# Order of the gates, the recurrence and the item table in a mixer and expert layer

## The reference

```
mod = silu(c) @ ada_w + ada_b                      # 1024 x 6144, six rows of 1024
z   = rmsnorm(x) * (1 + sc1) + sh1
xa, ya, u, v = split(z @ w_in, 4)                  # each 1024 x 512
xc  = causal_conv4(xa) + conv_b
r, i = sigmoid(xc @ wr + br), sigmoid(xc @ wi + bi)   # per head of 64 channels
a   = exp(-8 * r * softplus(-lambda))
h_t = a_t * h_(t-1) + sqrt(1 - a_t^2) * i * xc     # scan over the 1024 tokens
o_lru = h * gelu(ya)
o_sgu = gelu(u) * (W_causal @ layernorm(gelu(v)) + b)
h   = x + g1 * (concat(rmsnorm(o_lru), rmsnorm(o_sgu)) @ w_out)
z2  = rmsnorm(h) * (1 + sc2) + sh2
top4, gates = router(z2)
moe = sum over the four experts e of gate * (swiglu(z2 @ w_gu[e]) @ w_down[e])
out = rmsnorm(h + g2 * moe)
```

## Time and profile before

| what | us |
|---|---|
| median of 3 runs (lowest to highest) | 2106.76 (2106.14 to 2109.04) |
| the profiled run, whole | 2113.14 |
| its span, first to last instruction | 2111.4 |
| TensorE busy | 1947.7 (92%) |
| TensorE busy from 0 to 50 / 50 to 100 us | 14.92 / 46.92 |
| TensorE busy from 150 to 200 / 200 to 250 us | 42.42 / 43.13, granted clock 0.93 / 0.90 |
| TensorE busy from 450 to 500 / 500 to 550 us | 28.32 / 38.23, granted clock 0.79 / 0.86 |
| VectorE, ScalarE, GpSimd busy | 1007.5, 355.6, 536.5 |
| VectorE's first part of the table, end (`places_made`) | 479.4 |
| moved by DMA | 527.20 MB, mean 250 GB/s; from 0 to 54.68 us 329 GB/s |

### The profile page before, as it was taken

How to read it: one execution, slowest core, us unless ns; L and a number is a source line. 1 busy time by engine, 2 the same in 40 slices (tenths; PEclk the granted TensorE clock), 3 DMA queues, 4 the chain that set the end, 5 groups by cost and what they waited for, 6 DMA issues and landing times.

```text
span 2111.4 us, 53224 instructions
## 1 busy us (share of the span) xinstructions
PE 1947.7 (92%) x20253; PEld 805.0 (38%) x20254; DVE 1007.5 (48%) x2278; ACT 355.6 (17%) x729; POOL 536.5 (25%) x536
## 2 busy tenths in 40 slices
PE   3998999986889989999999999999999999999994
PEld 2443444441333424334343333343333333334332
DVE  6427756334534434544454544545444454454444
ACT  3024411221111111101010111111111111111012
POOL 2000022112232232322222323323333233322231
PEclk9998999997999999999999999999999999999997
DMA  9332135323492591959696969789898898999985
GB/s 327 137 119 80 40 120 172 153 92 130 131 362 83 185 358 25 347 201 337 208 332 214 376 252 389 274 329 359 283 392 287 305 354 285 389 397 356 332 297 180
DMA packets 128957, 527.20 MB, mean 250 GB/s; under 512 B 17184, under 2 KB 47920, under 8 KB 79760
## 3 DMA queue, kind: packets, MB, share of 16 engines
q1 hardware_dynamic: 95344, 470.39, 57.8%
q0 software_dynamic: 33568, 56.29, 11.5%
HBM read 494.22 MB, written 32.38 MB: 249 GB/s over the span
## 4 chain that ended last, share of the span: by engine, by line
PE 72%; DMA 15%; DVE 5%; SPq 4%; ACT 2%; issue 1%; POOL 1%; DVEq 0%; ACTq 0%; POOLq 0%
PE psum L1198 38%; PE psum L1218 20%; DMA big<-in_exp_w_gu_dram 10%; PE psum L1115 5%; PE psum L959 5%; DMA big<-in_exp_w_down_dram 2%; PE psum L1052 2%; SPq L487 1%; DMA big<-in_w_in_dram 1%; PE psum L999 1%; SPq L497 1%; DVE big L1409 1%; PE psum L1159 1%; SPq L468 0%; SPq L494 0%
## 5 line engine op out<-in xcount | busy, mean ns | idle before, releaser
L1198 PE MATMUL psum<-big,r 128*32 128x512 f32 x9152 | 1011.4, 599 | 39.1 <-DMA big<-in_exp_w_gu_dram 28.3
L1198 PEld LDWEIGHTS psum<-big,r 128*32 128x32 f32 x9152 | 291.4, 111 | 711.4 <-issue 649.9
L1218 PE MATMUL psum<-big,r 128*32 128x256 f32 x9152 | 511.1, 383 | 10.2 <-DVE r L1838 8.0
L689 POOL DMA_INDIRECT acc_rows<-r,scatter_idx x143 | 226.9, 1587 | 858.3 <-DVE r L1848 830.1
L1218 PEld LDWEIGHTS psum<-big,r 128*32 128x32 f32 x9152 | 293.9, 111 | 206.0 <-DVE r L1838 11.1
L870 ACT ACTIVATE r<-r,shift 128x128 f32<-128x128 f32 x376 | 154.2, 481 | 912.8 <-PE psum L1198 852.7
L678 POOL DMA_INDIRECT r<-hs_rows,gather_idx x192 | 223.7, 1165 | 87.7 <-issue 45.8
L1845 DVE TENSOR_TENSOR r<-psum,r 128x256 f32<-128x256 f32 x143 | 60.8, 425 | 288.0 <-PE psum L1218 287.0
L1823 DVE TENSOR_TENSOR r<-psum,r 128x256 f32<-128x256 f32 x143 | 60.4, 422 | 270.8 <-PE psum L1198 270.8
L959 PE MATMUL psum<-r,big 128*128 128x512 f32 x384 | 167.7, 597 | 3.1 <-DMA big<-in_w_in_dram 3.1
L1776 DVE STREAM_TRANSPOSE r<-r 128x1024 f32<-128x1024 f32 x47 | 97.6, 2076 | 107.8 <-issue 107.8
(11 more groups left out here) (286 smaller groups left out, 927.9 us busy)
## 6 DMA issues: line engine op xcount, KB each, us to landing
big<-in_exp_w_gu_dram SPq DMA_DIRECT2D x256, 1024.0 KB
big<-in_exp_w_down_dram SPq DMA_DIRECT2D x128, 1024.0 KB
big<-in_ada_w_dram SPq DMA_DIRECT2D x12, 2048.0 KB, 12.9
r<-in_x_dram SPq DMA_DIRECT2D x16, 512.0 KB, 12.7
big<-in_w_in_dram SPq DMA_DIRECT2D x4, 2048.0 KB, 20.2
r<-in_exp_b_gu_dram SPq DMA_DIRECT2D x128, 64.0 KB
big<-in_w_out_dram SPq DMA_DIRECT2D x2, 2048.0 KB, 13.4
hs_rows<-r POOLq DMA_DIRECT2D x8, 512.0 KB, 2.9
```

The source lines that it names most:

```text
L689: pool.indirect_dma_start(acc_quarters, bass.IndirectOffsetOnAxis(ap=scatter_idx[:, u:u + 1], axis=0), y_sb[:, u, :], None, bounds_check=4 ...
L1198: last = pe.matmul(psum[32 * j:32 * j + 32, u, :].rearrange("p (a n) -> p a n", a=2), izT[:, k, u * UNIT:(u + 1) * UNIT], rhs[:, :, 256 * ...
L1218: ins_ = pe.matmul(psum[32 * i:32 * i + 32, 4 + u % 2, 0:256], actT[:, u, f, :], down_slab(f)[:, 256 * i:256 * i + 256], start=(f == 0), s ...
```

## The change

Two stretches are written in another order, and the table chain gets shorter. No product of TensorE's main work is added or removed.

**Front.** The eleven small parameter loads go from SyncE's queue to ScalarE's. The gates' weights get a semaphore of their own (`gatew_in`) and, with all other mixer parameters of GpSimd's queue, are issued after `zT`, where before most of them were issued behind the third block of products. The two stores of zeros go behind the masking of `wmT`. `gates(0)` stands behind the second pair of `xa` projections, `gates(1)` behind the fourth, `gates(2)` behind the second pair of `ya`, `gates(3)` behind the fourth. The scan writes to `xaT` and no longer to `lru_t`, and the product with `ya` is a step of its own (`apply`), so that the recurrence doesn't need `ya`.

**Way in.** `make_places` comes ahead of the first unit's products. The second part of the table chain starts right after it, with the transpose of unit 0 behind its first four instructions; three sums at a time are taken with one instruction over a three-part tile, so that the chain has 33 instructions with the transpose among them, where it had 42 without it. `make_items` comes after the first unit's last pass. The table is copied out before the transposes of units 1 to 3. TensorE loads two of four registers later, waits for only one half of the modulated rows, and makes list 4 before `first_2b`. In the loop `make_onehot` comes right behind `block_rows`.

The diff, cut to its core:

```
@@ bank_jobs @@
+    for m in range(CT):
+        jobs += [("xa", (m, th), "dve") for th in range(2)]
+        if m % 2:
+            jobs += gates(m // 2)
...
     for ct in range(CT):
         jobs += [("ya", (ct, th), "act") for th in range(2)]
-        if ct >= 1:
-            jobs += gates(ct - 1)
+        if ct % 2:
+            jobs += gates(2 + ct // 2)
@@ SyncE: the loop over PARAM_ROWS goes away; ScalarE gets it as its first work @@
+            for name, rows in PARAM_ROWS:
...
+                act.dma_start(prow[ROW[name]:ROW[name] + rows, :], src.rearrange(pat, p=P)).then_inc(param_in, SEMW)
@@ GpSimd @@
-            pool.wait_ge(gemv_made, 3)
+            pool.wait_ge(filled, JOB[("zT", (KT - 1, 1))] + 1)
             for s in range(2):
                 for bd, w in ((wr_bd, "lru_wr"), (wi_bd, "lru_wi")):
...
-                                   ins[w][0].rearrange("(c s) i o -> s i c o", s=2)[s]).then_inc(mixpar_in, SEMW)
+                                   ins[w][0].rearrange("(c s) i o -> s i c o", s=2)[s]).then_inc(gatew_in, SEMW)
@@ TensorE @@
+            for m in range(CT):
+                for th in range(2):
+                    project("xa", ("win", 0), m, th)
+                if m == 1:
+                    pe.wait_ge(gatew_in, SEMW * 4)
+                if m % 2:
+                    gates(m // 2)
...
+            make_places()
             pe.wait_ge(first_made[0], 1)
-            gate_and_linear(0, 0, first=True, between=lambda k: make_places() if k == 0 else None)
+            gate_and_linear(0, 0, first=True)
             pe.wait_ge(first_made[1], 1)
-            gate_and_linear(0, 1, first=True, between=lambda k: make_items() if k == 2 else None)
+            gate_and_linear(0, 1, first=True, between=lambda k: make_items() if k == 3 else None)
             pe.wait_ge(items_ready, 1)
...
+            load_word(0, 1)
+            pe.reg_alu(units, loaded[1], 1, ALU.max)
+            pe.reg_mov(arrived, SEMW)
+            pe.wait_ge(z_made[0], 1)
...
             by_units(pe, units, 3, first_3b)
+            make_list(4, release=(freed[3],))
             by_units(pe, units, 2, first_2b)
-            make_list(4, release=(freed[3],))
+            repeat_rows(4)
             by_units(pe, units, 1, first_1b)
@@ VectorE, recurrence @@
-                link(dve.tensor_tensor_scan(lru_t[:, 0, :], lru_t[:, 3, :], lru_t[:, 2, :], 0.0, ALU.mult, ALU.add))
-                dve.tensor_tensor(yaT[:, ct, :], yaT[:, ct, :], lru_t[:, 0, :], ALU.mult).then_inc(lru_made, 1)
+                dve.tensor_tensor_scan(xaT[:, ct, :], lru_t[:, 3, :], lru_t[:, 2, :], 0.0, ALU.mult, ALU.add
+                                       ).then_inc(lru_made, 1)
...
+            copy_xa(0)
+            conv(0)
+            mod_products(4)
+            copy_xa(1)
+            mod_products(5)
+            recurrence(0)
+            conv(1)
+            copy_xa(2)
+            copy_xa(3)
...
+            recurrence(1)
+            conv(2)
+            mod_products(6)
+            apply(0)
+            apply(1)
+            recurrence(2)
+            conv(3)
+            apply(2)
+            mod_add(6)
+            mod_products(7)
+            recurrence(3)
+            apply(3)
@@ VectorE, table: one of the two sums over a three-part tile @@
+            link(dve.tensor_tensor(chosen, at_place, mask.unsqueeze(1).broadcast_to([P, 3, NE]), ALU.mult))
+            link(dve.tensor_reduce(sums_b, chosen, AX.X, ALU.add))
@@ VectorE, loop @@
                 block_rows(g + 1)
+                make_onehot(g + 3)
                 rows_here(g + 4, step)
                 make_idx(g + 2, step)
                 make_gates(g + 2, step)
-                make_onehot(g + 3)
```

More of the change, by code:

```diff
@@ L97, in bank_jobs @@
         if m == 0:
-            jobs += gates(CT - 1) + [("mod", 7, "dve")]
+            jobs += [("mod", 7, "dve")]
         if m == 2:
@@ L992, in _ @@
                 last.then_inc(filled, 1)
-            def gates(ct):
-                pe.wait_ge(conv_made, ct + 1)
-                for name, w in (("rec", wr_bd), ("inp", wi_bd)):
-                    for th in range(2):
-                        b = open_bank(name, (ct, th))
-                        pe.matmul(b, w[:, ct, :], lru_t[:, 0, th * 512:(th + 1) * 512], start=True, stop=True
-                                  ).then_inc(filled, 1)
             def sum_squares(grp, th):
```

157 lines of the change are left out of this document (72 added, 85 removed).

## The result

The changed kernel takes 2078.39 us, the median of four runs (2070.52 to 2079.87), beside 2106.45 (2105.9 to 2109.04) for the kernel before, four runs on the same chip. The ratio of the two is 0.985, 95% interval 0.983 to 0.987. Forecast were 2074.0 us, range 2067 to 2083. On two other chips the ratio came out at 0.985 and 0.985 again.

A forecast was written before the change was run, and what follows sets the result against it. TensorE, busy 92% of the span, was taken as the bound, so only its waits and starts pay. 22.2 + 2.5 + 3.4 + 4.7 = 32.8 us off the median 2106.8 gave 2074.0 us, range 2067 to 2083.

The forecast's parts named there:

- Front: Projections to the end of u: gates stop waiting, 14.5 us of waits and 7.7 of slowed passes go, 22.2 us gained.
- slow passes: In the front, gate passes and the last pair of u run slower after waits; 7.7 us expected to go with the waits.
- Opening: Start to first projection: w_in leaves the path, VectorE's chain starts sooner; gain 2.5 us, between a loss of 1.1 and 3.8.
- rule of turns between rings: Parameter loads at the start: DMA engines alternate between rings packet by packet, so landing is small and the sum 1.3 us better.
- Way in to unit 1: From the first unit to unit 1's first pass: no wait in `make_items`, four modulations awaited instead of eight; 3.4 us gained.
- rule of the exclusive lock: Table chain beside GpSimd's gates: shared SBUF ports held for a whole instruction; by it alone the 3.4 us gain could be 0.
- First down product: Behind unit 1's start: earlier list 4 and one-hot matrix, register loads overlapped; 4.7 us gained, 2.7 if loads don't overlap.
- Loop: Items of the loop: earlier one-hot matrix counts 0, since TensorE then waits for the next expert's weights; at best 4 us.
- rival E: Loop: gathers late because indices come 1.5 us later, 70 us over 47 items, less 33: 2144 us; chance 0.03.
- A: Front: a wait stays because a round takes 8 to 12 us longer than 21.9; 2081 us for one; chance 0.08.
- F: Front's waits are replaced by equal ones, only the start and the way in gain: 2096 us; chance 0.03.
- C: Way in doesn't move: GpSimd holds VectorE's chain or register loads aren't hidden; 3.4, 2.0 or 8.1 us lost, 2079 to 2082; chance 0.12.

The follow-up runs named there:

- way in alone: Kernel before with only the new way in and the new order in the loop, front as before: 2108.0 us beside 2112.63, ratio 0.9971.
- order undone: Changed kernel with the one-hot matrix back behind indices and gates in the loop: 2077.28 us, ratio 0.983, where the changed kernel had 2082.64.
- order alone: Kernel before with only the one-hot matrix put ahead of rows, indices and gates in the loop: 2107.85 us against 2108.23, ratio 1.0002.
- first silu ahead: Changed kernel with the old order in the loop and an early silu on one column: 2075.3 us, ratio 0.983, beside 2077.61 of the changed kernel.

## Why the prediction was right

**Front, 22.2 forecast, 23.6 measured** (184.70 or 184.71 us in ten traces, against 208.33, 208.52 and 210.05 in the three with the front of before; these three wait 14.5 us each, so what scatters is the slow passes, 9.2 to 10.8 us). The mechanism is the one given: rounds that fit into the spacings. The convolutions ended at 99.8, 131.3 and 164.2 us, the gates wanted them at 110.1, 143.6 and 175.4: 10 to 12 us early, as said. `apply(1)` made VectorE wait 6.0 us for ScalarE, and nobody was held. The waits were sized to 0.05 us. The term that was mis-sized is the slow passes: 9.18 instead of 7.7, since I had listed four groups of rows and other passes behind the waits were slow too; it passes the upper end I gave, 23, by 0.6. Behind u 0.7 to 0.9 us were lost again, where the forecast kept the shift whole (26.65 us ahead at the end of u, 25.7 at the first list, in the first trace); 0.6 of it are TensorE's three waits for GpSimd in the spatial unit, 4.7 us where they were 4.1.

**Opening, 2.5 forecast, 2.8 measured** (51.9, the mean of three traces, against 54.68). The parameters landed at 9.6, 4.5 us after their last issue; taken were 10, and 13.4 as the worst. By the Trainium skill's rule of turns between rings, which the prediction cited, the landing would be small and the sum 1.3 us better. The landing of 9.6 is nearer to that than to 13.4, and brought 0.5 of the 1.3 (products at 11.99 instead of the 12.5 forecast). Two things I didn't see: of the 2.4 us counted from the landing to the first product 1.28 are a load of ScalarE's table of functions, which can run earlier, and w_in needed only one of the two edits.

**Way in to unit 1, 3.4 forecast, 3.8 to 4.1 measured** (26.80 us from the first list to unit 1's start before, 22.72, 23.01 and 23.01 in the three traces after; the other two kernels with the old way in have 26.75 and 26.87). The place of the product carries about half of it, and `make_items` waits no more, as said. The chain's length was wrong by 1.8 us: forecast end 9.3 us behind the product of the places (479.7 to 489), measured 464.83 - 453.78 = 11.05. It still ended 1.2 us ahead of TensorE's 64 passes, so the error cost nothing. Of GpSimd's 6.6 us the chain lost 2.8, where I had 3.8, and 6.6 as the worst: five instructions took 3.97 us that take 1.17 elsewhere, and each ends within 0.12 us of the end of one of GpSimd's. Two of them, and GpSimd beside them:

```profile
460.25 0.86 DVE L1753 TENSOR_TENSOR g1row<-g1row 128x1 f32<-128x1 f32 x1
461.15 1.11 DVE L1754 TENSOR_SCALAR g1row<-iota_e,g1row 128x3 f32<-128x3 f32 x1
```

```profile
460.24 0.85 POOL L704 TENSOR_TENSOR big<-big,r 128x256 f32<-128x256 f32 x1
461.16 1.07 POOL L705 CAST r<-big 128x256 bf16<-128x256 f32 x1
```

By the Trainium skill's rule of the exclusive lock, cited in the prediction, each two-input instruction could have waited for a whole one of GpSimd's. The first of these two did, and so did the second, which has one tensor input (two of the five are of this kind). But this two-input instruction, in the middle of a cast of GpSimd's, was not held:

```profile
457.45 0.32 DVE L1739 TENSOR_TENSOR g1row<-g1row 128x96 f32<-128x96 f32 x1
```

```profile
457.03 1.06 POOL L701 CAST r<-big 128x256 bf16<-128x256 f32 x1
```

Most of the others ran at 0.15 to 0.32 us too. So the worst case by that rule, gain 0, didn't come, and what decides which of them wait was not found out.

**First down product, 4.7 forecast, 4.2 measured in the first trace, 3.3 and 3.6 in the others** (from unit 1's start to TensorE's restart 44.66 before; 40.46, 41.32, 41.09 after). With S the start of unit 1, VectorE's transposes start at S + 20.8, where I had S + 20.5 and before it was S + 24.0, and the activation at S + 26.8 (forecast 26.1, before 30.8). The term that was mis-sized is the overlap of the register loads: their 1.98 us of issue are gone, but 1.13 stand ahead of the activation, where I had 0.5. In the two kernels with this way in and the loop's order undone the distance is 41.80 and 41.52, with first passes of unit 1 as fast as in the first trace, so this edit is worth 1.1 to 1.3 of the 2.0 that hung on the overlap. In the other two traces unit 1's first passes took 5.97 instead of 5.34 us besides.

**Loop, 0 forecast.** Means of 1520.8 and 1519.8 us: no difference that can be told, for the reason that the prediction gave, the transfers of the next weights. I left it for a while when the first two traces showed 3.5 us there, and paid with four missed expectations (way in alone, order undone, order alone, first silu ahead). The gathers moved 1.5 us closer to their use, as reckoned: the last one ends its issue at 573.95, the rows are used at 581.74, 7.8 us later instead of 9.3, and VectorE doesn't wait for them. That disposes of rival E. A and F did not come either, since no gate waits; of C only the part of the register loads came, some 0.6 us.

**Sum.** 32.8 forecast; up to the restart 32.8 to 34.0 measured. That the sum fits better than its terms is luck: they were off by +1.4 (front), +0.2 to +0.5 (opening), -0.7 to -0.9 (behind u), +0.4 to +0.7 and -0.5 to -1.4 (way in), and these cancel. The medians give 28.1, 30.0 and 30.6, the ratios of 0.985 some 31 to 33 with an interval of 4 to 5 either way. The loop scatters by 14 us over the traces, and a single profiled run of before stands for its opening and its first down product; the 1 to 5 us between traces and medians stay open. The two profiled runs are the extremes, 2113.14 us above all four timed runs of before in that series and 2070.52 the fastest of after, so their difference of 42.6 us is no measure of the gain. The base did not decide the forecast: from the median it gave 2074.0, 4.4 us too low; from the profiled run it would have given 2113.1 - 32.8 = 2080.3, 1.9 too high, in range as well.

## What to carry to other kernels

Make a periodic chain fit before shortening it: write beside each round of the engine that is waited for the work that the waiting engine has meanwhile. Here much the same instructions in another order gave 23.6 us, and ten instructions fewer in a chain gave nothing. Credit a difference between two traces only up to the first point where a transfer sets the time; behind it compare several executions of each kernel, or the same edit on two bases. A place where one engine waits less is worth nothing if the next thing it needs is a transfer that was set off earlier.

## What the runs showed that I had not expected

- From the first projection to the end of u TensorE took 184.70 or 184.71 us in ten executions in which it never waited there. Behind its waits for weights the same passes lose 0, some 1.7 or some 3 us, differently in each execution.
- Eleven small loads on a queue of their own, beside blocks of 2 MB on another, landed 4.4 to 4.6 us after their last issue in nine of ten traces, and in one after 5.4 us (TensorE's wait for them ended at 10.72 instead of 9.5 to 9.8).
- Behind 1290 us, six of the ten traces with the early one-hot matrix show the passes of some items of three units 0.4 to 0.6 us longer (21.3 instead of 20.8), none of the four with the late one. It costs under 3 us in a run and does not show in the means; I did not settle its cause. All six come from two of the chips, on which the two traces with the late matrix don't show it; three of the four early traces without it come from a third chip. So the order alone is not the cause.
